# Attention: the next group's first query tile, projected ahead of and between the maxima

## The reference

```python
q_x, k_x, v_x = jnp.split(h_x @ w_qkv, [qd, qd + kvd], axis=-1)
q_x = rope_2d(rms_norm(q_x.reshape(B, S, N_HEADS, HEAD_DIM), q_gain), tables)
...
s_ctx = jnp.einsum('bqkgd,bnkd->bkgqn', qb, k_c) * scale
s_loc = jnp.where(valid, jnp.einsum('bqkgd,bnkd->bkgqn', qb, kb) * scale, NEG_INF)
p = jax.nn.softmax(jnp.concatenate([s_ctx, s_loc, sink_col], axis=-1), axis=-1)
o = p[..., :L] @ v_c + p[..., L:L + band] @ vb
out_x = o_x @ w_o
```

## Time and profile before

| | us |
|---|---|
| median of 3 runs | 3534.88 |
| lowest and highest | 3523.78, 3536.03 |
| span of the profiled execution | 3537.2 |
| TensorE busy in it | 3277.9 (93%) |
| attention's four groups, first maximum to last score | about 162 to 577 |

### The profile page before, as it was taken

The page is one execution under the profiler, slowest core; times in us unless marked ns, Lnnn a source line. Parts: engine busy times, 40 slices in busy tenths (PEclk is TensorE's granted clock), DMA queues, the critical chain, the costliest instruction groups (busy, mean ns, idle before and its releaser), DMA issues.

```text
span 3537.2 us, 38584 instructions
## 1 busy us (share of the span) xinstructions
PE 3277.9 (93%) x15192; PEld 2485.8 (70%) x15192; DVE 1807.9 (51%) x2302; ACT 1312.9 (37%) x2009; POOL 1676.6 (47%) x872
## 2 busy tenths in 40 slices
PE   9899888999999999999899998988899899788996
PEld 2666555888888768778588886645677675467776
DVE  3645555653231632332411115466699663767995
ACT  3332324311111422222332223253388431534883
POOL 1433332544443433324355553353499643535994
PEclk9989979999999999999999999998999999999998
DMA  9100001444432112212223331212489622126994
GB/s 353 32 24 18 18 12 58 138 143 144 150 124 86 59 48 66 66 42 78 86 87 100 97 96 54 72 60 85 167 287 314 218 73 78 36 85 210 398 315 148
DMA packets 119603, 417.61 MB, mean 118 GB/s; under 512 B 12928, under 2 KB 17536, under 8 KB 118528
## 3 DMA queue, kind: packets, MB, share of 16 engines
q1 hardware_dynamic: 92640, 324.05, 27.5%
q10 hardware_dynamic: 22176, 74.32, 5.8%
q0 software_dynamic: 4608, 16.78, 1.3%
HBM read 403.04 MB, written 46.66 MB: 127 GB/s over the span
## 4 chain that ended last, share of the span: by engine, by line
PE 67%; DVE 21%; ACT 5%; POOL 3%; issue 2%; DMA 2%; ACTq 0%; DVEq 0%; SPq 0%; POOLq 0%
PE PS L104 67%; DVE RT L116 4%; DVE WL L116 4%; DVE SCR L116 2%; DVE SCR L128 2%; DVE SCR L122 1%; ACT RT L110 1%; ACT SCR L110 1%; POOL WL L116 1%; ACT WH L110 1%; DVE SM L131 1%; DVE XF L122 1%; POOL RT L116 1%; DVE BF L128 1%; DVE XF L116 1%
## 5 line engine op out<-in xcount | busy, mean ns | idle before, releaser
L104 PE MATMUL PS<-RT,WH 128*128 128x512 f32 (+1 forms) x5728 | 1547.0, 372 | 61.0 <-DVE RT L122 26.0
L104 PEld LDWEIGHTS PS<-RT,WH 128*128 128x128 f32 x5728 | 1045.1, 192 | 309.5 <-issue 52.2
L116 POOL TENSOR_TENSOR WL<-RAW,WH 128x1024 fp32r<-128x1024 f32 x306 | 769.8, 2517 | 944.4 <-ACT WH L110 944.2
L104 PE MATMUL PS<-RT,WL 128*128 128x512 f32 (+1 forms) x2864 | 939.7, 369 | 0.0
L110 ACT ACTIVATE WH<-RAW 128x1024 fp32r<-128x1024 f32 x324 | 340.8, 1055 | 663.6 <-PE PS L104 580.6
L104 PEld LDWEIGHTS PS<-RT,WL 128*128 128x128 f32 x2864 | 501.4, 193 | 58.9
L116 POOL TENSOR_TENSOR RT<-SCR,RT 128x512 fp32r<-128x512 f32 (+2 forms) x178 | 235.0, 1326 | 534.8 <-ACT RT L110 359.3
L104 PE MATMUL PS<-WH,RT 128*128 128x256 f32 (+1 forms) x1528 | 389.4, 335 | 15.8 <-DVE RT L116 14.8
L116 DVE TENSOR_TENSOR SCR<-PS,SCR 128x256 f32<-128x256 f32 (+1 forms) x128 | 67.7, 543 | 497.3 <-PE PS L104 468.4
L104 PEld LDWEIGHTS PS<-WH,RT 128*128 128x128 f32 x1528 | 263.1, 191 | 48.5 <-DVE RT L116 21.0
L104 PE MATMUL PS<-BF 128*128 128x512 f32 (+2 forms) x612 | 265.1, 612 | 6.0 <-ACT XF L110 4.2
(11 more groups left out here) (194 smaller groups left out, 3903.4 us busy)
## 6 DMA issues: line engine op xcount, KB each, us to landing
BF<-in_moe SPq DMA_DIRECT2D x152, 512.0 KB, 5.2
RAW<-in_ff SPq DMA_DIRECT2D x132, 512.0 KB
BF<-in_ada SPq DMA_DIRECT2D x96, 512.0 KB, 5.1
RAW<-in_ret SPq DMA_DIRECT2D x64, 512.0 KB
RAW<-in_moe SPq DMA_DIRECT2D x64, 512.0 KB
XF<-in_moe SPq DMA_DIRECT2D x60, 512.0 KB, 7.6
BF<-placed_in ACTq DMA_DIRECT2D x46, 512.0 KB, 6.9
placed_out<-BF ACTq DMA_DIRECT2D x46, 512.0 KB, 8.8
```

Of the source, the lines that this page charges most:

```text
L104: return NOTHING if self.e is None else self.e.matmul(o, w, x, start=first, stop=last)
L116: return NOTHING if self.e is None else self.e.tensor_tensor(*a)
```

## The change

In groups 1 and 2 the next group's first query tile is projected in two halves: blocks 0 to 3 ahead of maximum 0, blocks 4 to 7 behind it. In group 0 its eight blocks stand one by one behind the maxima 5, 7, ... 19. Group 3 has no next group. ACT's and DVE's work on that tile moves with it in groups 1 and 2 (on DVE behind reduction 3, on ACT ahead of the sinks). In group 0 they stay behind the maxima. The waits of the banks follow, and the weights are stacked in the new order of use. No instruction's kind or size is changed, and none is added or taken away on TensorE.

```diff
             for g in range(4):
+                if 0 < g < 3:
+                    pe_next_head(pe, g, 0, range(0, 4))
                 for it in range(24):
                     pe_max(pe, g, it)
+                    if 0 < g < 3 and it == 0:
+                        pe_next_head(pe, g, 0, range(4, 8))
+                    if g == 0 and 4 <= it < 20 and it % 2:
+                        pe_next_head(pe, 0, 0, range(it // 2 - 2, it // 2 - 1))
                     if g and it >= 5 and it % 2 and (it - 5) // 2 < OUT_EARLY[g - 1]:
                         pe_att_out(pe, g - 1, (it - 5) // 2)
-                if g < 3:
-                    pe_next_head(pe, g, 0)
...
-        def pe_next_head(pe, g, m):
+        def pe_next_head(pe, g, m, ks):
             key = ("q", 2 * g + 2 + m)
-            for j in range(2):
-                if m:
-                    pe.wait_ge(*dve_done.at(("hq1", ("q", 2 * g + 2), j)))
-                    pe.wait_ge(*act_done.at(("hrr", ("q", 2 * g + 2), 1)))
-                elif g:
-                    pe.wait_ge(*dve_done.at(("x", "att", g - 1, j, 7)))
-            pe_head(pe, key, [PS[:, 6, :], PS[:, 7, 0:L]])
+            if ks[0] == 0 and (g or m):
+                for j in range(2):
+                    pe.wait_ge(*dve_done.at(("hq1", ("q", 2 * g + 1 + m), j)))
+                    if m and g:
+                        pe.wait_ge(*dve_done.at(("x", "att", g - 1, j, 7)))
+                pe.wait_ge(*act_done.at(("hrr", ("q", 2 * g + 1 + m), 1)))
+            pe_project_to(pe, [PS[:, 6, :], PS[:, 7, 0:L]], key, 8, XP, h_pair, h_ready("att"), ks)
...
             elif m == 1:
                 for j in range(2):
-                    pe.wait_ge(*dve_done.at(("hq1", ("q", 2 * g + 3), j)))
+                    pe.wait_ge(*dve_done.at(("hq1", ("q", 2 * g + (4 if g < 2 else 3)), j)))
...
             for g in range(4):
+                if 0 < g < 3:
+                    act_head(act, ("q", 2 * g + 2))
                 for blk in range(6):
                     act_sink(act, g, blk)
...
-                if g < 3:
-                    act_head(act, ("q", 2 * g + 2))
+                if g == 0:
+                    act_head(act, ("q", 2))
...
                     dve_max(dve, g, it)
+                    if 0 < g < 3 and it == 3:
+                        dve_head(dve, ("q", 2 * g + 2))
...
-                if g < 3:
-                    dve_head(dve, ("q", 2 * g + 2))
+                if g == 0:
+                    dve_head(dve, ("q", 2))
...
-                           *[b for g_ in range(4) for b in (
-                               [_mk(qkv[:, 256 * g_ + 256:256 * g_ + 512])] if g_ < 3 else []) + [
-                               _mk(wo[256 * g_:256 * g_ + 256])]]], 0))
+                           _mk(qkv[:, 256:512]),
+                           *[b for g_ in range(2) for b in (
+                               _mk(qkv[:, 256 * g_ + 512:256 * g_ + 640]), _mk(wo[256 * g_:256 * g_ + 256]),
+                               _mk(qkv[:, 256 * g_ + 640:256 * g_ + 768]))],
+                           _mk(wo[512:768]), _mk(wo[768:1024])], 0))
```

More of the change, by code:

```diff
@@ L894, in pe_head, with pe_project_to @@
             pe_project_to(pe, outs, key, 8, XP, h_pair, h_ready("att"))
-        def pe_project_to(pe, outs, key, kt, parts, x, ready):
-            for k in range(kt):
+        def pe_project_to(pe, outs, key, kt, parts, x, ready, ks=None):
+            for k in ks or range(kt):
                 w = next_block(pe)
@@ L1147, in pe_att @@
                     if g < 3 and t == 8:
-                        pe_next_head(pe, g, 1)
+                        pe_next_head(pe, g, 1, range(8))
                     if g < 3 and t == 11:
```

## The result

| | before | after |
|---|---|---|
| median of 20 runs, us | 3535.2 | 3518.9 |
| lowest and highest | 3512.86, 3540.5 | 3508.47, 3526.8 |
| span of the profiled execution | 3537.2 | 3509.7 |

The ratio is 0.996, with an interval of 0.995 to 0.997. The change takes off 16.3 us, 0.46%. That lies within the bound of no change that the prediction set (17.7 us), and it is real, since the interval excludes 1. Of the runs of the kernel before that stand beside the experiments, one slow run of 9665.8 us is left out.

The account below looks back on a forecast made before the run. TensorE was taken to bound the kernel, holding 67% of the chain. Terms of +7.0, -8.6, -0.6, -8.6 and -0.5 us summed to -11.3 us, 3525.9 against the 3537.2 span; forecast for the median 3524 us, range 3508 to 3538.

Parts of the forecast that it names:

- Groups 1 and 2: Both groups gain: -8.6 us each behind the maxima, and -0.6 and -0.5 us ahead of them.
- the -9.4: End of group 1: the first score could start at 308.65 instead of 318.08, right after the last reduction, -9.4 us.
- the +0.4 of the case with a low clock at the first output projection: Front of group 1: maximum 6 starts at 282.4 against 281.99 if that projection runs at half clock, +0.4 us.
- The first scores at the low clock: First score tiles of groups 0 to 2: the clock may be low there, +0.8 us each, between 0 and 2.5.
- The 4.0 us for maxima 1 to 5: Start of groups 1 and 2: these maxima go at DVE's pace, in about 4.0 us.
- POOL in time: Group 1's front: POOL's fold and first queries end at about 277.0, just when reduction 3 ends, before DVE's take-out.
- Group 0: Blocks moved among low-clock maxima make group 0 longer by +7.0 us, between +5 and +9.
- A pair of maxima with its block at the low clock: Group 0's maxima: a block costs 2.03 us at the low clock, read from group 3; eight cost 16.3 us.
- The waits that the blocks absorb: Group 0, up to maximum 19: blocks lie over waits for the reductions, some 0.7 us in all.
- Group 0 at full clock: Rival: blocks among group 0's maxima raise its clock, so it gives -6 instead of +7: 3510.5 us, chance 0.10.
- Slower, with groups 1 and 2 low: Rival: low clock from the first output projection, +19 us per group; one: 3543, chance 0.11; both: 3562, chance 0.05.
- the level of group 3: Forecast kept group 3's maxima low; the rival raised them, -8.9 and perhaps -0.6 us, to 3514.5 us, chance 0.30.

Follow-up runs that it names:

- e10: The changed kernel itself measured again, beside e9 on one chip: 3517.6 us, ratio 0.9961 to the kernel before.
- e4: The changed kernel, but group 0's blocks stand two at a time behind maxima 5, 7, 9 and 11: 3511.2 us, ratio 0.9945.
- e1: The changed kernel without its part in group 0, whose projection stands behind the maxima as before: 3511.7 us, ratio 0.9945.
- e3: The changed kernel, but all eight of group 0's blocks stand behind maximum 1, where TensorE idles: 3502.8 us, ratio 0.9922.
- e9: The kernel of e3 measured again, beside the changed kernel on another chip: 3505.2 us, ratio 0.9930.
- e7: Group 0 as in e3; against e3, groups 1 and 2 have all eight blocks ahead of maximum 0: 3519.0 us, one run.
- e2: The kernel before with only the change's group 0 part, eight single blocks behind maxima 5 to 19: 3539.5 us, ratio 1.0016.
- e6: e3 with output projections 0 and 1 together behind maximum 5 in groups 1 to 3, none behind maximum 7: 3507.8 us, ratio 0.9925.
- e8: e3, but groups 1 and 2 have four blocks ahead of maximum 0, two behind it, two behind maximum 2: 3501.8 us, ratio 0.9926.

## Why the prediction was right, and where it was off

The forecast was 3524 us, the range 3508 to 3538 us, and no change by 0.5% was given the greatest chance. The measured 3518.9 us is in the range and the change is 0.46%. By steps:

- **Groups 1 and 2: right in mechanism, group 1's match partly luck.** Predicted -9.2 and -9.1 us, measured -9.2 and -10.2 between the table loads in the trace, and -9.2 and -7.9 in e10's. But 1.6 and 1.0 us of the first two, and 1.6 and 0.5 of e10's, lie in the score tiles ahead of the first block. What the prediction added up came to -7.6 and -9.2 us, and to about -7.5 us each in e10. The end of group 1: the first score moved from 9.52 to 0.26 us behind the last reduction, -9.3 us, as the -9.4 said. The front of group 1: 17.1 us from TensorE's release to maximum 6 against 16.8, the +0.4 of the case with a low clock at the first output projection (its first blocks ran so). The front of group 2, at full speed, took 15.8 against 16.7: -0.9 where -1.5 was expected. The first scores at the low clock cost 1.2 and 1.0 us where 0.8 was taken. The 4.0 us for maxima 1 to 5 held (3.85 us, 280.93 to 284.78), but the place it was read from says something else: 272.93 to 277.91 are 4.98 us for maxima 2 to 5, at the low clock.
- **POOL in time: right.** Fold and queries came as before, and DVE's take-out began without a wait.
- **Group 0: right in sign, too large.** Predicted +7.0, measured +5.6, +3.4 and +3.5 in three executions, two of them below the stated bound of +5. A pair of maxima with its block at the low clock, the price that carried the sum, was sized right: with four matmuls in each maximum it took 4.92 us (180.58 to 185.50 in the trace of after), 2.9 for the maxima and 2.0 for the block. The waits that the blocks absorb were taken too small: maxima 16 to 19 now need 0.51 us a pair (206.06 to 206.57) instead of the 1.1 or more that the reductions had dictated. And the clock rose at the seventh or eighth block, where the forecast had all eight at the low level. In the trace of after it was low again for part of the first scores (8.0 us before and 9.2 after, up to the table load), 1.2 us for the 0.8 in the sum; in e10's this was 0.2 us.
- **Group 0 at full clock, the rival by the Trainium skill's rule** (TensorE: Matmul & The Clock Gate, "Part 1: The HAM clock gate": activity releases the throttle): refuted for the change by 0.52 over the stretch. The rule itself is not contradicted. e4 has the same blocks in pairs, and rose behind the first pair. (The rival's own terms, -8 and -5 us, give 3511 us, not 3510.5.)
- **Slower, with groups 1 and 2 low:** not seen in the two traces of the changed kernel, nor in e1, e3, e4 and e9, which have the same order there. The first output projection of group 1 did run low in both traces of the changed kernel, and that of group 2 in one, but the clock rose again behind it each time.
- **The step that was off is the last one, the level of group 3.** "So I take the median to be a run with one such group, as the trace is." In the profiled execution of the changed kernel and in e10's, no group stayed low. The term of -9.5 us for group 3 was right (measured -9.8 and -9.5); the choice to leave it out of the forecast was not well founded. Of the ten traces here in which group 3's order is that of the kernel before, three have it low (before, e4, e7) and seven don't. In the order of the kernel before, group 3 was low in one trace (before) and group 2 in another (e2). The changed kernel had none low in two traces out of two, and of the six traces with its order in groups 1 to 3 one had group 3 low (e4), which is too few for a rate. Forecast and rival, 3524 and 3514.5 us, lie on the two sides of 3518.9, and the twenty runs, from 3508.5 to 3526.8, cover both. The medians moved by 16.3 us where the sum said 11.3. How the other 5 us divide between group 3's level and the shorter low stretches in the score tiles isn't shown, as only one of the twenty runs has a trace.

## What to carry to other kernels

An operation that is moved gains what it leaves, minus what it costs where it arrives. Here the same eight blocks were worth -6.3 to -7.8 us in a wait of 9 to 10 us that was there already (e3, e6, e8, e9; -3.1 in e7, where DVE was late behind it), and +3.4 to +5.6 us between operations that ran at the low clock. Look for the longest wait of the engine that bounds and ask whether the work can be ready for it, before interleaving. And where a level of the clock differs between executions of one kernel, compare several executions or stage by stage: a single pair of traces said -27.5 us here, and twenty runs said -16.3.

## What the runs showed of the hardware

- One and the same order of instructions stayed at 1.2 GHz for 30 us and more in one execution (e4's group 3, 0.50 from 485 to 515 us) and ran at 2.4 GHz in another, and this was worth 8 to 10 us in a group. The clock fell behind four or five short maxima in a row (e6 and e7, the change). In the ten traces with the output projections in their old places, it rose behind the first two blocks of the output projection, or sooner, in 26 of the 30 groups 1 to 3. In the other four (group 3 of before, e4 and e7, group 2 of e2) it stayed low for another 25 to 35 us, with pairs of maxima and pairs of blocks taking turns.
- Four subtractions on DVE between two tensors took 6.50 us in e3 and 8.17 us in the trace of after, at the same place and with the same operands (`BFR<-SCR,BFR`, 64 partitions by 768). That set the wait ahead of maximum 2 to 10.26 us instead of 8.59, and explains most of the 2.0 us by which the trace of after was late before the change begins. It is the third of the four that differs, and POOL began a fold (`RT<-BF,RT`) within 0.01 us of it. In nine of the twelve traces the third subtraction took 0.95 us and POOL's fold 2.6; in the other three (after, e6, e8) they took 2.62 and 1.81. So one of the two was held up by the other, now this one and now that. e7's small operations above fit this. No experiment kept the two engines apart. DVE in order of time, first e3:

```profile
156.88 6.50 DVE L116 TENSOR_TENSOR BFR<-SCR,BFR 64x768 fp32r<-64x768 f32 x4
```

and the kernel after:

```profile
156.71 8.17 DVE L116 TENSOR_TENSOR BFR<-SCR,BFR 64x768 fp32r<-64x768 f32 x4
```
